# One ScalarE copy per weight tile for the high halves in the three FFNs, GpSimd left with the low halves

## What is computed

```python
def swiglu(h, w_gate, w_up, w_down):               # FFN1 and FFN2, inner width 2816
    return (silu(h @ w_gate) * (h @ w_up)) @ w_down

x = x + 0.5 * g1 * swiglu(modulate(rms_norm(x), sh1, sc1), ...)      # FFN1
x = x + g2 * (gate_a * fourier(...) + gate_b * mla(...)) @ w_out
x = rms_norm(x + 0.5 * g3 * swiglu(modulate(rms_norm(x), ...), ...)) # FFN2
x = x + gt1 * rms_norm(attention_2(...) @ w_out_2)
y = square(relu(h @ w_up_2)) @ w_down_2            # FFN3, inner width 4096
x = x + gt2 * rms_norm(y)
```

## Time and profile before

| | us |
|---|---|
| median of 3 runs | 2119.05 |
| lowest and highest run | 2113.77 and 2120.78 |
| the profiled execution | 2122.36 |
| its span, first to last instruction | 2120.6 |
| its mean granted TensorE clock | 0.950 of full speed |

### The profile page before, as it was taken

One profiled execution on the slowest core, in us unless ns is written; L12 is line 12 of the kernel. 1 busy time (PEld: TensorE's weight loads), 2 busy tenths in 40 slices (PEclk: granted clock), 3 DMA queues, 4 the chain that ended last, 5 costly groups with the idle time before them and its releaser, 6 DMA issues.

```text
span 2120.6 us, 25191 instructions
## 1 busy us (share of the span) xinstructions
PE 1960.8 (92%) x8956; PEld 1532.7 (72%) x8956; DVE 1225.9 (58%) x1834; ACT 364.1 (17%) x749; POOL 1154.1 (54%) x1075
## 2 busy tenths in 40 slices
PE   5999999979999998899999968985999969999997
PEld 3788888867667887688888847664666748788785
DVE  7888378645644133887078365676775267405714
ACT  2100000012145111200000021111555220000001
POOL 3577767746530676576677742565000328767761
PEclk8999999989999999899999979896999989999997
DMA  8554555422210224454365232233000112233221
GB/s 271 189 180 161 183 167 174 154 72 87 62 60 1 80 81 126 137 171 137 113 193 174 82 67 40 62 80 100 1 1 1 38 42 80 98 99 94 91 93 40
DMA packets 231131, 216.51 MB, mean 102 GB/s; under 512 B 20305, under 2 KB 227342, under 8 KB 231054
## 3 DMA queue, kind: packets, MB, share of 16 engines
q1 hardware_dynamic: 230000, 214.84, 32.9%
q10 hardware_dynamic: 1054, 0.66, 0.1%
HBM read 213.39 MB, written 2.10 MB: 102 GB/s over the span
## 4 chain that ended last, share of the span: by engine, by line
PE 85%; DVE 11%; issue 2%; ACT 1%; DMA 0%; ACTq 0%; POOL 0%; DVEq 0%; POOLq 0%; SPq 0%
PE ps L613 24%; PE ps L614 23%; PE ps L615 23%; PE ps L877 4%; PE ps L900 4%; PE ps L886 2%; DVE rb L1414 1%; PE ps L655 1%; DVE sq_sum L1410 1%; DVE tt L1908 1%; DVE tt L1631 1%; DVE xT L1909 1%; PE ps L644 1%; PE ps L684 1%; DVE score L1792 1%
## 5 line engine op out<-in xcount | busy, mean ns | idle before, releaser
L524 POOL TENSOR_TENSOR w_lo<-raw,w_hi 128x512 fp32r<-128x512 f32 (+2 forms) x612 | 799.3, 1336 | 12.8
L613 PE MATMUL ps<-h_hi,w_hi 128*128 128x512 f32 x1424 | 569.3, 400 | 34.0 <-DVE h_lo L1436 27.0
L614 PE MATMUL ps<-h_lo,w_hi 128*128 128x512 f32 x1424 | 561.1, 394 | 0.0
L615 PE MATMUL ps<-h_hi,w_lo 128*128 128x512 f32 x1424 | 560.5, 394 | 0.0
L517 POOL TENSOR_TENSOR w_hi<-raw,ones 128x8 fp32r<-128x8 f32 x153 | 34.4, 225 | 913.0 <-PE ps L615 861.7
L613 PEld LDWEIGHTS ps<-h_hi,w_hi 128*128 128x128 f32 x1424 | 271.7, 191 | 101.1 <-issue 37.3
L1443 DVE SCALAR_TENSOR_TENSOR ada_sum<-ada,cT,ada_sum 128x256 f32<-128x256 f32 x378 | 322.8, 854 | 13.4
L614 PEld LDWEIGHTS ps<-h_lo,w_hi 128*128 128x128 f32 x1424 | 271.6, 191 | 58.9 <-issue 3.0
L615 PEld LDWEIGHTS ps<-h_hi,w_lo 128*128 128x128 f32 x1424 | 271.1, 190 | 57.8
L613 PE MATMUL ps<-g_hi,w_hi 128*128 128x512 f32 x608 | 240.8, 396 | 3.1 <-ACT sg L1373 3.1
L614 PE MATMUL ps<-g_lo,w_hi 128*128 128x512 f32 x608 | 240.2, 395 | 0.0
(11 more groups left out here) (272 smaller groups left out, 2266.5 us busy)
## 6 DMA issues: line engine op xcount, KB each, us to landing
ada<-in_ada_w SPq DMA_DIRECT2D x31, 1024.0 KB, 5.5
ada<-in_w_ada SPq DMA_DIRECT2D x24, 1024.0 KB, 6.9
raw<-in_ffn_w_gate SPq DMA_DIRECT2D x22, 1024.0 KB, 7.3
raw<-in_ffn_w_up SPq DMA_DIRECT2D x22, 1024.0 KB, 5.3
raw<-in_w_in SPq DMA_DIRECT2D x16, 1024.0 KB, 5.3
raw<-in_w_up SPq DMA_DIRECT2D x16, 1024.0 KB, 5.4
raw<-in_w_down SPq DMA_DIRECT2D x16, 1024.0 KB, 5.2
raw<-in_ffn_w_down SPq DMA_DIRECT2D x16, 768.0 KB, 4.5
```

The lines of the kernel that those rows point to most:

```text
L524: last = pool.tensor_tensor(lo[:, c], src[:, c], hi[:, c].bitcast(F32), ALU.subtract)
L613: pe.matmul(o, wh, xh, start=start, stop=False)
L614: pe.matmul(o, wh, xl, start=False, stop=False)
L615: return pe.matmul(o, wl, xh, start=False, stop=stop)
```

## The change

In the loops of the three FFNs the high half of a weight tile is made by ScalarE, in one copy of the whole tile (`split_high`), and GpSimd waits for it and makes only the four low quarters (`split_low`). The first two tiles of each FFN keep the old `split` on GpSimd, outside the loop; so do all tiles between the FFNs. Because the first iteration's two tiles need no ScalarE copy, its Silus or Relus are taken out of the loop and stand ahead of it. In each loop body ScalarE's order is: high half of the tile u = 0, high half of the tile u = 1, then the Silus or Relus of this iteration. The loops over the down tiles are new on ScalarE; they stand between the Silus or Relus and whatever ScalarE did next, in the second half the squares of the norm.

```diff
@@ GpSimd
+        def split_low(n, kc, cols, i, per):
+            size = kc * cols
+            src, hi, lo = (t[:, n % 2, 0:size] for t in (raw, w_hi, w_lo))
+            pool.wait_ge(hi_done, i * per + (n + 1))
+            quarter = size // 4
+            for q in range(4):
+                c = slice(q * quarter, q * quarter + quarter)
+                last = pool.tensor_tensor(lo[:, c], src[:, c], hi[:, c].bitcast(F32), ALU.subtract)
+            last.then_inc(split_done, 1)
@@ split_down
-                    split(n0 + u, kc, 256, j, 2)
+                    split_low(n0 + u, kc, 256, j, 2)
@@ FFN1 and FFN2
+                elif it0 == 0:
+                    split(n0, NC, 256)
+                    split(n0 + 1, NC, 256)
-                with pool.Fori(1 if n0 == 0 else 0, iters) as it:
+                with pool.Fori(1 if it0 == 0 else 0, iters) as it:
                     for u in range(2):
-                        split(n0 + u, NC, 256, it, 2)
+                        split_low(n0 + u, NC, 256, it, 2)
@@ FFN3
-            with pool.Fori(0, 4) as it:
+            if half == 0:
+                split(n0, NC, 256)
+                split(n0 + 1, NC, 256)
+            with pool.Fori(1 - half, 4) as it:
                 for u in range(2):
-                    split(n0 + u, NC, 256, it, 2)
+                    split_low(n0 + u, NC, 256, it, 2)
@@ ScalarE
+        def split_high(n, kc, cols, i, per):
+            size = kc * cols
+            act.wait_ge(raw_in[n % 2], i * (8 * per) + arrived[n])
+            act.wait_ge(hi_done, i * per + n)
+            act.wait_ge(tile_used, i * per + (n - 1))
+            act.copy(w_hi[:, n % 2, 0:size], raw[:, n % 2, 0:size]).then_inc(hi_done, 1)
@@ ScalarE, FFN1 and FFN2
-                with act.Fori(0, iters) as it:
+                def silus(it):
                     for m in range(2):
                         act.wait_ge(tile_used, it * 2 + (n0 + 1))
                         ...
+                if half == 0:
+                    silus(0)
+                with act.Fori(1 - half, iters) as it:
+                    for u in range(2):
+                        split_high(n0 + u, NC, 256, it, 2)
+                    silus(it)
+                with act.Fori(0, 4) as j:
+                    for u in range(2):
+                        split_high(n0 + 2 * iters + u, iters, 256, j, 2)
             norm_squares(act, (1, 3)[i], x_ready, (X_F1B, X_F2B)[i], xT)
@@ ScalarE, FFN3
-            with act.Fori(0, 4) as it:
+            def relus(it):
                 for j in range(4):
                     u, m = j // 2, j % 2
                     act.wait_ge(tile_used, it * 2 + (n0 + u + 1))
                     ...
+            if half == 0:
+                relus(0)
+            with act.Fori(1 - half, 4) as it:
+                for u in range(2):
+                    split_high(n0 + u, NC, 256, it, 2)
+                relus(it)
+            with act.Fori(0, 4) as j:
+                for u in range(2):
+                    split_high(n0 + 8 + u, NC, 256, j, 2)
         norm_squares(act, 7, y_ready, 16, y2)
```

## The result

| | before | changed |
|---|---|---|
| median of the runs, us | 2117.03 (4 runs) | 2227.98 (4 runs) |
| lowest and highest, us | 2113.77 and 2120.78 | 2224.31 and 2232.19 |
| span of the profiled execution, us | 2120.6 | 2225.9 |
| mean granted clock | 0.950 | 0.936 |

The changed kernel is slower by 111 us: the ratio is 1.0526, with a 95% interval of 1.0505 to 1.0547. 2232 was forecast, with a range of 2207 to 2246.

What follows compares the result with a forecast made beforehand. TensorE was taken to bound the kernel, no split being waited for. FFN3 stalls 69.7, FFN ends 16.4 and half clock 27 us sum to 113 us: 2235 us on the profiled execution, 2232 on the median, range 2207 to 2246.

Steps and rivals of the forecast that it cites:

- 8 stalls in FFN3: At each FFN3 iteration's end TensorE waits 9.1 us, the next copy standing behind Relus j = 2, 3; 69.7 us net.
- 3 stalls at the ends of the FFNs: Before down tile 6, squares queue behind the last copy and hold VectorE: 5.0, 5.0 and 6.4 us, together 16.4 us.
- half clock after 11 stalls: After each new stall TensorE runs 5.2 us at half clock, losing 2.44 us; 27 us together.
- The bound: FFNs run at TensorE's pace; it waits for no split in the loops, so a faster split gains nothing.
- The copy: ScalarE's high-half copy takes 1.9 us for 2048 columns, bounds 1.0 and 2.5 us, and 1.25 us for 1280.
- The rival by which ScalarE gets ahead of its waiting Relus: In FFN3 the high half is ready in time, no stall: time stays at 2119 us, or 2117; chance 3%.
- The low half in the stall: GpSimd's low half in an FFN3 stall takes 5.55 us, between 5.05 with VectorE idle and 6.16 beside its squares.
- the last step: From release to TensorE's next matmul, in FFN3's stalls and at the FFN ends: 0.43 us.
- The part ahead of the low half: In an FFN3 stall, two Relus 1.1 us, copy 1.9 us and hand-overs 0.1 us: low half starts after 3.1 us.
- The slack of 2.2 us in the gate tiles: In FFN1 and FFN2, Silus, copy and low half take 8.7 of 10.95 us, so gate tiles cost nothing.
- a little quicker: VectorE may run slightly faster with less company from GpSimd; TensorE waits for it nowhere in these loops.

Runs made afterwards that it cites:

- both places mended: Changed kernel with FFN3's u = 0 copies right after Relus j = 0, 1 and the norm squares between the down-tile copies: 2115.90 us, ratio 0.9997 to the kernel before.
- two-copies kernel: Changed kernel with each ScalarE copy made twice, first into the low slot, then into the high slot: 2238.04 us, ratio 1.0572 to the kernel before.
- kernel with the busy TensorE: Changed kernel with 38 more matmuls, read by nobody, after tile u = 1 of each FFN3 iteration: 2215.04 us, ratio 1.0453 to the kernel before.
- late split: Kernel before, GpSimd's FFN3 splits of tiles u = 0 and the first down tile made to wait for all four preceding Relus: 2211.25 us, ratio 1.0449.
- squares moved: Changed kernel with each FFN's norm squares placed after the copies for down tiles 3, 5 and 7, two chunks each: 2208.39 us, ratio 1.0432 to the kernel before.

## Why the prediction was right, point by point

| term | forecast us | measured us |
|---|---|---|
| 8 stalls in FFN3, less 3.1 us from before | 69.7 | 73.4 - 3.1 = 70.3 |
| 3 stalls at the ends of the FFNs | 16.4 | 9.5 + 6.1 = 15.6 |
| half clock after 11 stalls | 27 | 28 |
| sum | 113 | 114 |
| medians, changed less before | 113 | 111 |

- **The bound.** TensorE's waits, read before anything else, said that no split is waited for. With both places mended the relief of GpSimd is there in full, and the time is that of the kernel before to 0.1%. This part rests on an experiment.
- **The copy.** Taken at 1.9 us and, for 1280 columns, 1.25 us from a slope over two other shapes; measured 1907 ns in 70 copies and 1264 ns in 16.

```profile
L1211 ACT CAST w_hi<-raw 128x2048 fp32r<-128x2048 f32 x70 | 133.5, 1907 | 319.4 <-PE ps L632 319.2
```

- **The stalls in FFN3.** Eight, at the places named; 9.22 us (six) and 9.03 us (the two into the down tiles) for 9.1. The rival by which ScalarE gets ahead of its waiting Relus did not occur: in every iteration the copy follows the second pair of Relus, although it could have run a whole tile earlier. The trace agrees with the Trainium skill ("TensorE: Matmul & The Clock Gate", Architectural detail: the array is 16× 32×32, not 1× 128×128), by which that queue is strictly first in, first out.
- **The low half in the stall, and the last step.** Here two misses cancel. The low half was taken at 5.55 us, between 5.05 and 6.16; it took 5.99, near the upper end. The last step was taken at 0.43 us from the earlier trace rows, where TensorE waits for ScalarE; from the end of GpSimd's fourth quarter (1799.73 + 5.99 = 1805.72) to the matmul at 1805.97 it took 0.25. The part ahead of the low half took 2.98 us for 3.1. So 2.98 + 5.99 + 0.25 = 9.22 us, for 3.1 + 5.55 + 0.43 = 9.1. In the two-copies kernel, where the low half starts later, it took 4.96 us. That its length depends on how much of VectorE's work is still to come was right; the place between the bounds was not.
- **The ends.** 4.8, 4.7 and 6.1 us for 5.0, 5.0 and 6.4. The steps named (copy, square, sum, chunk 2, sum, chunk 3) are in the trace one after the other. Most of the difference is again the last step: from the end of chunk 3, 1230.20 + 0.74, to the matmul at 1231.17 it took 0.23 us instead of 0.43. VectorE's sum in FFN2 took 0.68 us instead of 0.80. Its first copy in FFN3 took 1.06 us; I had taken 0.95.

```profile
1231.17 0.70 PE L630 MATMUL ps<-g_hi,w_hi 128*128 128x512 f32 x1 [4.74 <-DVE xT L1546]
```

- **The clock.** 5.2 us low for each, measured 5.4 in the mean over the 11, from 3.4 to 6.2. The 28 us of the table are these lengths at the prediction's 0.47, not a time that was measured by itself. That the low clock is a cost of its own rests on the kernel with the busy TensorE, 20.5 us in FFN3, where the same working gives 8 x 5.7 x 0.47 = 21.5.
- **What the sum leaves out.** The profiled spans differ by only 105.3 us, the medians by 111. FFN3's stretch alone grew by 102.0 us, of which the stalls and their low clock explain 100. Up to FFN3 the two waits of FFN1 and FFN2 and their low clock add 9.5 + 4.2 us, yet the changed kernel's profiled execution reached FFN3 only 3.8 us later: the rest, the same instructions, took about 10 us less. Here too the clock goes with it. It was low for 184 us before FFN3 in the kernel before and for 170 in the changed one, although 10 of the 170 are new. A forecast made against one profiled execution carries that scatter.
- **A step that was not seen.** The slack of 2.2 us in the gate tiles was worked out with Silus of 1.1 us "as the Relus do". In the kernel before, an instruction that the trace names ACT_TABLE_LOAD stood ahead of both Silus in each of the six iterations of the first half of FFN1, and likewise in FFN2. With it the slack would have been 0.9 us. The changed kernel has 15 of these loads and no longer 25: with the new loop form only the first Silus of either FFN have one. The forecast of nothing for the gate tiles would have held with the loads too, but with much less to spare than it says. Which part of the new loop form removed them no run separates. Before, then changed:

```profile
113.30 1.28 ACT L1195 ACT_TABLE_LOAD   x1 [20.30 <-PE ps L615]
114.60 1.09 ACT L1195 ACTIVATE sg<-ps 128x512 f32<-128x512 f32 x2
```

```profile
113.72 1.09 ACT L1220 ACTIVATE sg<-ps 128x512 f32<-128x512 f32 x2 [9.91 <-PE ps L632]
114.69 1.91 ACT L1211 CAST w_hi<-raw 128x2048 fp32r<-128x2048 f32 x1
```

## What to carry to other kernels

When work moves to an idle engine, ask not how much it does but what it will be waiting for when the new work becomes possible. A copy that must run beside the present tile may not stand behind an instruction that waits for the end of that tile; it belongs right behind one that waits for what the copy itself waits for. Here that is the end of the tile u = 0, which the Relus j = 0, 1 wait for and which frees the slot. Look at the waits of the engine that bounds the kernel first: if none of them names the engine that is relieved, the move has little to win. Here its best outcome was no change, and it reached that only after both queues were reordered.

## What was not expected of the hardware

**VectorE's company.** In FFN1, from 270 to 370 us, VectorE did the same 98 instructions in 82.45 us before and in 60.28 us after, with GpSimd's busy time down from 71.65 to 46.83 us. Before, then changed (us, then busy of TensorE, its loads, VectorE, ScalarE, GpSimd):

```profile
270.00:370.00 100.00, 100.00 (x458) 83.38 (x457) 82.45 (x98) 5.45 (x10) 71.65 (x63) 1.00 0.57 181
```

```profile
270.00:370.00 100.00, 100.00 (x459) 83.35 (x457) 60.28 (x98) 21.40 (x19) 46.83 (x36) 1.00 0.58 182
```

ScalarE's copies of the same data slow VectorE much less than GpSimd's high passes did. The same instruction shows it by what runs beside it: VectorE's step of ada on 128x256 (L1443, L1488) in FFN1, from 100 to 420 us, took 478 ns in the mean beside no work of GpSimd's, 790 ns where nine tenths of it or more fell beside GpSimd's high passes and 1238 ns beside its low quarters, all in the kernel before; in the changed kernel it took 485 ns beside a copy of ScalarE's (31 of them) and 469 ns beside neither. I had called it "a little quicker"; it is a quarter. TensorE waits for none of this work in the loops, so it was worth nothing here. Whether it would decide in a kernel bound by VectorE is not shown.

**A longer idle time may cost less than its length.** At each of the eight stalls the low clock lasted 10.2 us from its fall to its return, in the changed kernel and in the one with two copies alike. What is spent of it while TensorE is idle is not spent on matmuls. That is why, by the working above, the second copy cost 0.1 us a stall and not 0.8, and why a term for the clock can't simply be added to a stall whose length changes. The 10.2 us are no constant: with the late split, seven of the eight stalls had them and one, of 10.5 us like its neighbours, had 13.7; with the squares moved, the last of the eight, of 9.0 us, had 6.8. So the 0.1 us holds for these places and is no rule.
